# Prompt rows of the experts taken by eight, and the last norm moved into the last expert

## The reference

```
aff  = softmax(h @ router)                       # every token, 16 experts
gate, idx = top_k(aff^T, 2 * t / 16)             # each expert takes 128 of 1024 sample tokens,
                                                 #   16 of 128 prompt tokens
xe   = h[idx]
hid  = silu(xe @ e_gate) * (xe @ e_up)           # 1024 -> 2816
ye   = (hid @ e_down) * gate                     # 2816 -> 1024
x    = x + gt2 * zeros.at[idx].add(ye)
y    = x * rsqrt(mean(x * x) + eps) * final_norm_g
```

## Time and profile before

| | us |
|---|---|
| median of 3 timed runs | 3868.48 (3867.92 to 3871.03) |
| profiled execution | 3860.96 |
| its span, first to last instruction | 3859.2 |

### The profile page before, as it was taken

The page is one execution under the profiler, slowest core; times in us unless marked ns, Lnnn a source line. Parts: engine busy times, 40 slices in busy tenths (PEclk is TensorE's granted clock), DMA queues, the critical chain, the costliest instruction groups (busy, mean ns, idle before and its releaser), DMA issues. The chain is left out here.

```text
span 3859.2 us, 81746 instructions
## 1 busy us (share of the span) xinstructions
PE 3562.1 (92%) x37038; PEld 3101.1 (80%) x37038; DVE 1231.4 (32%) x3103; ACT 671.1 (17%) x1677; POOL 192.0 (5%) x150
## 2 busy tenths in 40 slices
PE   5899899999899979289999999999999999999995
PEld 2387685959555545189999999999999999999995
DVE  3376767777444443701111111111111111111112
ACT  2323324242144532100000000000000000000001
POOL 0010101010000000000000000000000000000000
PEclk7899999999999999589999999999999999999997
DMA  7200000000121022098887878788787878878773
GB/s 323 61 16 10 15 5 20 4 19 4 27 79 31 18 72 94 21 354 292 274 266 263 267 259 273 261 273 268 265 267 258 273 262 269 268 268 269 258 251 110
DMA packets 498393, 664.38 MB, mean 172 GB/s; under 512 B 31183, under 2 KB 437095, under 8 KB 494975
## 3 DMA queue, kind: packets, MB, share of 16 engines
q1 hardware_dynamic: 492238, 640.23, 49.5%
q0 software_dynamic: 5632, 18.88, 1.9%
q10 hardware_dynamic: 176, 0.05, 0.0%
HBM read 630.70 MB, written 28.36 MB: 171 GB/s over the span
## 5 line engine op out<-in xcount | busy, mean ns | idle before, releaser
L2094 PE MATMUL bank<-e_hid,e_wd 128*128 128x144 f32 x5632 | 760.1, 288 | 0.0
L2082 PE MATMUL bank<-e_xT,e_wg 128*128 128x144 f32 x5632 | 749.5, 286 | 1.0 <-ACT e_xT L2136 1.0
L2082 PE MATMUL bank<-e_xT,e_wu 128*128 128x144 f32 x5632 | 748.1, 286 | 0.0
L2082 PEld LDWEIGHTS bank<-e_xT,e_wg 128*128 128x128 f32 x5632 | 715.5, 190 | 1.0 <-issue 1.0
L2094 PEld LDWEIGHTS bank<-e_hid,e_wd 128*128 128x128 f32 x5632 | 710.5, 190 | 5.6
L2082 PEld LDWEIGHTS bank<-e_xT,e_wu 128*128 128x128 f32 x5632 | 714.4, 190 | 0.0
L2179 DVE TENSOR_TENSOR e_tm<-bank,e_sg 128x144 f32<-128x144 f32 x352 | 108.3, 308 | 1853.0 <-ACT e_sg L2143 1853.0
L2143 ACT ACTIVATE e_sg<-bank 128x144 f32<-128x144 f32 x352 | 102.2, 290 | 1998.4 <-PE bank L2082 1998.4
L532 PE MATMUL bank<-hT_x,wblk 128*128 128x512 f32 (+1 forms) x672 | 237.5, 511 | 14.5 <-DMA wblk<-in_w_in 8.5
L532 PEld LDWEIGHTS bank<-hT_x,wblk 128*128 128x128 f32 x672 | 114.1, 197 | 130.4 <-issue 112.4
L727 PE MATMUL bank<-r_TW,r_X 64*64 64x64 f32 x2880 | 167.5, 220 | 4.3 <-DVE r_X L1198 1.3
(11 more groups left out here) (324 smaller groups left out, 3469.9 us busy)
## 6 DMA issues: line engine op xcount, KB each, us to landing
e_wg<-in_e_gate SPq DMA_DIRECT2D x176, 1024.0 KB, 5.5
e_wu<-in_e_up SPq DMA_DIRECT2D x176, 1024.0 KB, 8.1
e_wd<-in_e_down SPq DMA_DIRECT2D x176, 1024.0 KB, 11.0
h_wmod<-in_w_mod SPq DMA_DIRECT2D x24, 1024.0 KB, 17.1
wblk<-in_w_in SPq DMA_DIRECT2D x22, 512.0 KB
h_x<-in_x_sample SPq DMA_DIRECT2D x8, 512.0 KB, 6.6
wo<-in_w_out SPq DMA_DIRECT2D x2, 2048.0 KB, 11.6
o_x<-in_x_sample SPq DMA_DIRECT2D x8, 512.0 KB, 4.2
```

The source lines that it names most:

```text
L2082: last = nc.tensor.matmul(bank[6 + b % 2][:, j * TOK:(j + 1) * TOK], w[s][:, k, f], xT[e % 2][:, k, :], start=(k == 0), stop=(k == KD - 1))
L2094: last = nc.tensor.matmul(bank[k // PER_BANK][:, c:c + TOK], wd[s][:, b % DUO, k * P:(k + 1) * P], hid[:, b % 2, :], start=(b == 0 and k % ...
```

## The change

- `topk` treats the prompt first; SP writes its indices and gates to HBM and loads them back as two columns of 128 (`idxq`, `gateq`): rows of eight experts one below the other.
- The prompt rows are gathered 128 at a time (`gather_prompt`, for experts 0 to 7 and 8 to 15), transposed once into `xpT` (`prompt_token`), and VectorE copies each expert's 16 columns into its `xT` (in `tokens`).
- On the way back `collect` copies an expert's 16 prompt columns into `ypT`; for experts 0 to 7 and 8 to 14 these are turned together (`prompt_output`, in expert 8 and expert 15) and scaled together (`prompt_scaled`). Each expert's 16 rows are still added by a scatter of their own, in a row, each waiting for the one before (`scatter_prompt`).
- Token numbers 0 to 127 compared with the last expert's prompt indices give a 16x128 matrix `pick`; its product with the last expert's 16 prompt rows is added to the prompt tile in place of a scatter.
- The stage `final` is gone. In expert 15, while its products run, SP loads the eight sample tiles (without expert 15's sum) into weight buffers that are free, ScalarE squares them, VectorE norms them in place. POOL gathers the 128 rows that expert 15 chose. When its result is there, these rows are summed and normed, and after the eight tiles are stored they are stored over them by an indirect DMA.

The core of the diff (`topk`'s SP block, buffers, semaphores and the plain halves of changed pairs are left out):

```diff
+        GROUP = ((0, 8), (8, 15))
+        SQUARES = {14: (0, 1), 15: (2, 3), 16: (4, 5), 17: (6, 7)}
+        SCALES = {18: (0, 1), 19: (2, 3), 20: (4, 5), 21: (6, 7)}
...
 SP, behind the last weights:
+                sp.wait_ge(used, FIRST_FREE + 1)
+                sp.wait_ge(sc, 16 * LASTE)
+                for i in range(TILES - 1):
+                    if i == 6:
+                        sp.wait_ge(used, NEXT_FREE + 1)
+                        sp.dma_start(gf, ...).then_inc(gf_in, 16)
+                    sp.dma_start(fx[i], K.dram["ffn"][i * P:(i + 1) * P, :]).then_inc(fx_in[i], 16)
+                sp.wait_ge(scp, 16 * LASTE)
+                sp.dma_start(fx[8], K.dram["ffnp"][:, :]).then_inc(f8_in, 16)
+                for i in range(TILES - 1):
+                    sp.wait_ge(fy_ok, i + 1)
+                    sp.dma_start(A["y_sample"][0, i * P:(i + 1) * P, :], fx[i]).then_inc(fy_st, 16)
+                sp.wait_ge(py_ok, 1)
+                sp.dma_start(A["y_prompt"][0, :, :], fx[8]).then_inc(py_st, 16)
...
 POOL:
+                def scatter_prompt(e):
+                    if e:
+                        K.hold(pool, scp, 16 * e)
+                    pool.indirect_dma_start(out=K.dram["ffnp"][:, :], ..., in_=yp[part(e), :],
+                                            compute_op=ALU.add).then_inc(scp, 16)
...
+                    if e == LASTE:
+                        K.hold(pool, x_ps, NE)
+                        K.hold(pool, sc, 16 * LASTE)
+                        pool.indirect_dma_start(out=xe[:, :], in_=K.dram["ffn"][:, :], ...).then_inc(fr_in, 16)
+                    for g, (first, last) in enumerate(GROUP):
+                        if e == last + 1 or (e == last and last == NE - 1):
+                            K.hold(pool, sp_ok, 2 * g + 2)
+                            for i in range(first, last):
+                                scatter_prompt(i)
...
+                K.hold(pool, scp, 16 * LASTE)
+                K.hold(pool, fy_st, 16 * (TILES - 1))
+                K.hold(pool, zy_ok, 1)
+                pool.indirect_dma_start(out=A["y_sample"]..., in_=xe[:, :], ...).then_inc(patched, 16)
+                K.hold(pool, patched, 16)
...
 TensorE:
-                    nc.tensor.transpose(bank[b][:, c:c + CAP], xe[:, k * P:(k + 1) * P], K.ident[:, :])
-                    last = nc.tensor.transpose(bank[b][:, c + CAP:c + TOK], xp[:, k * P:(k + 1) * P],
-                                               K.ident[0:CAPP, 0:CAPP])
+                    last = nc.tensor.transpose(bank[3 + k // HALF][:, ...], xe[:, k * P:(k + 1) * P], K.ident[:, :])
...
+                        if e == GROUP[0][1] - 1 and b in (2, 3, 4, 5, 9, 10, 11, 12):
+                            prompt_token(1, b - 2 if b < 6 else b - 5, 5)
+                        for g, (first, last) in enumerate(GROUP):
+                            if e == last and b in (4, 5, 6, 7, 10, 11, 12, 13):
+                                prompt_output(g, b - 4 if b < 8 else b - 6)
...
+                for h in range(2):
+                    pe.wait_ge(sp_ok, 2 * len(GROUP) + h + 1)
+                    nc.tensor.matmul(bank[h][:, :], pick[:, :], yp[0:CAPP, h * 512:(h + 1) * 512], ...)
...
 VectorE, in block b of expert e:
+                        if e and b == YT + 2:
+                            collect(e - 1)
+                        for g, (first, last) in enumerate(GROUP):
+                            if e == last and b in (9, 15):
+                                prompt_scaled(g, b // 15)
+                        if e == LASTE:
+                            if b == 17:
+                                mean_square(slice(0, 8), fsq_ok, 8, fms_ok)
+                            if b == 18:
+                                reciprocal(slice(0, 8), frt_ok, frc_ok)
+                            for i in SCALES.get(b, ()):
+                                normed(fx[i], i).then_inc(fy_ok, 1)
...
 VectorE, behind the last expert:
+                V.tensor_tensor(xe[:, :], xe[:, :], ye[:, :], ALU.add).then_inc(z_ok, 1)
+                last_prompt_scaled(0)          # waits for scp at 16 * 15
+                last_prompt_scaled(1)
+                mean_square(slice(9, 10), zsq_ok, 1, zms_ok)
+                reciprocal(slice(9, 10), zrt_ok, zrc_ok)
+                normed(xe[:, :], 9).then_inc(zy_ok, 1)
```

More of the change, by code:

```diff
@@ new lines, in experts, with part @@
+        fx = [cell(n) for n in range(TILES)]
+        gf, fjunk = cell(TILES), [cell(TILES + 1), cell(TILES + 2)]
+        fst = sb("final_stats", [P, 4, TILES + 1])
+        number = sb("token_number", [CAPP, P], I32)
+        numf = sb("token_numberf", [CAPP, P])
+        lastf = sb("last_index", [CAPP, 1])
+        pick = sb("last_pick", [CAPP, P])
+        SQUARES = {14: (0, 1), 15: (2, 3), 16: (4, 5), 17: (6, 7)}
+        SCALES = {18: (0, 1), 19: (2, 3), 20: (4, 5), 21: (6, 7)}
+        def part(e):
+            return slice((e % 8) * CAPP, (e % 8 + 1) * CAPP)
@@ L2104, in output, with output_last_prompt @@
                         pe.wait_ge(yv_ok, e + 1)
[L2105 to L2110, removed]
-                        last.then_inc(y_ps, 1)
+                    last = nc.tensor.transpose(bank[3 + k // HALF][:, (k % HALF) * P:(k % HALF + 1) * P], yT[:, k, 0:CAP],
+                                               K.ident[:, :])
+                    if k % HALF == HALF - 1:
+                        last.then_inc(y_ps, 1)
+                def output_last_prompt(k):
+                    last = nc.tensor.transpose(bank[5 + k // HALF][0:CAPP, (k % HALF) * P:(k % HALF + 1) * P],
+                                               yT[:, k, CAP:TOK], K.ident[:, :])
+                    if k % HALF == HALF - 1:
+                        last.then_inc(yp_ps, 1)
                 for k in range(KD):
                     token(0, k)
+                for k in range(KD):
+                    prompt_token(0, k, 5 - 3 * (k // HALF))
                 gate_up(0, 0)
@@ L2220, in _ @@
                 scaled(NE - 1, 1)
[L2223 to L2277, removed]
-                    V.tensor_scalar(st[:, 1, i:i + 1], st[:, 0, i:i + 1], 1.0 / D, EPS, ALU.mult, ALU.add)\
-                     .then_inc(ms_ok, 1)
-                def out(i):
-                    dve.wait_ge(rt_ok, i + 1)
-                    V.reciprocal(st[:, 3, i:i + 1], st[:, 2, i:i + 1]).then_inc(rc_ok, 1)
-                    dve.wait_ge(rc_ok, i + 1)
-                    if i >= 4:
-                        dve.wait_ge(y_st[i % 4], 16 * (i // 4))
-                    V.scalar_tensor_tensor(y[i % 4][:, :], x[i][:, :], st[:, 3, i:i + 1], gf[:, :], ALU.mult,
-                                           ALU.mult).then_inc(y_ok, 1)
-                mean(0)
-                dve.wait_ge(rows, 16)
-                for i in range(TILES):
-                    if i + 1 < TILES:
-                        mean(i + 1)
-                    out(i)
@@ L2298, in trunk @@
+                for h in range(2):
+                    n = slice(h * 512, (h + 1) * 512)
+                    dve.wait_ge(pick_ps, h + 1)
+                    last = V.tensor_tensor(fx[8][:, n], fx[8][:, n], bank[h][:, :], ALU.add)
+                last.then_inc(p_ok, 1)
+                mean_square(slice(8, 9), psq_ok, 1, pms_ok)
+                reciprocal(slice(8, 9), prt_ok, prc_ok)
+                dve.wait_ge(p_ok, 1)
+                normed(fx[8], 8).then_inc(py_ok, 1)
 def trunk(nc, A):
```

207 lines of the change are left out of this document (177 added, 30 removed).

## The result

The changed kernel takes 3780.55 us (median of 4 runs, 3779.4 to 3781.19), the kernel before 3869.18 beside it (4 runs, 3867.92 to 3871.03): ratio 0.977, interval 0.9753 to 0.9787. That is 88.6 us faster, where 71.4 were forecast.

The account below looks back on a forecast made before the run. TensorE's issue was taken to bound the kernel from first to last product. Experts -55.5 + 2.6, start +1.0 and tail -19.5 sum to -71.4 us, from 3868.48 to 3797; range 3786 to 3828 (own range 3786 to 3806).

Parts of the forecast that it names:

- The bound: From first gate/up product to last down product, time is the sum of what TensorE issues; busy 800 of 800 us.
- E: End of the last down product, 3811.23 us in the profile before; the tail's times count from it.
- 1, TensorE in the experts: Expert loop: transposes removed give -55.5 us, added ones +2.6; an expert takes 131.2 us instead of 134.9.
- 2, the cover: Expert blocks: new VectorE and ScalarE work, squares and norms included, hides under 4.7 us of cover per block, costing nothing.
- 3, the start: Ahead of the first product: the larger prompt gather, transposes and copies cost +1 us (ends -0.5 and +3).
- 4, the tail: Behind the last down product: scatter chain, stores, patch scatter and exit take 28.5 us instead of 48.0, so -19.5.
- the step of the chain: Group 1's seven serial prompt scatters on POOL, each waiting for the one before: 5.5 us a step, low end 3.8.
- C: Scatter chain's end, forecast E + 1.1; also the rival: slow token transpose isn't the 16 rows' doing, 3820 or more, chance 0.07.
- The exit: POOL leaving a block at the end: 0.4 + 5.2 us, the 5.2 paid once in either kernel.
- A: Rival: POOL sees its own DMAs late, 10.8 us a scatter in the tail; 3834 us, chance 0.14.
- B: Rival: the scatter chain runs at the loaded loop's price, 8.5 us a step; 3818 us, chance 0.12.
- D: Rival: slower than before, serial scatters with every store behind them on SP; 3876 us at 16.6 a scatter, chance 0.02.

Follow-up runs that it names:

- experiment 2: Kernel before, each prompt token piece turned from all 128 rows by a product with 16 identity columns instead of a 16-row transpose: 3853.32 us, ratio 0.9962.
- experiment 1: Kernel before, with a small POOL memset behind its last wait in the experts and another as its first instruction of the next stage: 3867.86 us.
- experiment 3: Changed kernel with the old last stage behind the experts, expert 15's prompt rows scattered like the others, no early norms: 3804.64 us, ratio 0.984.
- experiment 6: Changed kernel with fourteen serial scatters, sample stores and chosen rows' norm no longer behind the chain, POOL's wait ahead of the patch dropped: 3796.49 us.
- experiment 4: Changed kernel with the eight sample squares, their statistics and norms put behind the last expert: 3796.81 us, ratio 0.982.
- experiment 7: Changed kernel with six weight duos loaded during top-k, `gt2`/`gt2p` first in the experts, ScalarE's root table loaded early: 3776.16 us, ratio 0.9765.
- experiment 8: As experiment 7, with `gt2` and `gt2p` loaded during top-k too: 3779.6 us, ratio 0.9774.
- experiment 9: The changed kernel again, with no edit: 3781.59 us, ratio 0.9774.
- experiment 5: Changed kernel with a second, zero-adding scatter behind each of group 1's seven prompt scatters, fourteen in a row: 3804.4 us, ratio 0.9838.

## Why the prediction was right or wrong

**The bound: right.** TensorE's issue sets the time from the first product to E. The clock stayed 1.00.

**1, TensorE in the experts: right.** -54.0 against -52.9. The samples' gathers of consecutive experts stand 131.15 us apart (131.2 forecast). The unrounded 0.353 for the 16-row transpose is shown by the changed kernel's blocks (6.35 to 5.99) and loop; experiment 2 shows that 0.09 of it is its neighbour's ahead. That the row count alone makes it dear was argued, not separated.

**2, the cover: right.** TensorE did not idle in expert 15. The last norm ended at E - 0.5 (forecast -0.4), ScalarE's table for the sigmoid was loaded again from 3736.86 on, 0.7 before it was needed. The bare price of squares and norms is 16.3 (20 forecast), since part of it finds other cover behind E.

**3, the start: too dear by 2.9 of -1.9 against +1.** Behind top-k's end the first transpose came at 9.8 (10.9 before), the last one ended at 13.5 (forecast 14.8), and the first product stood 1.6 behind that (forecast 3.1). The forecast added the larger gather to a time at which the old kernel had both kinds of rows; the new one starts on the sample rows as soon as they are there and the prompt's eight transposes follow 1.8 later. And it put all copies in a row behind the last transpose, where VectorE's first (1656.88) and ScalarE's lie beside the transposes; 1.6 are left behind them. The ends given, -0.5 and +3, missed it by 1.4.

**4, the tail: here the prediction failed**, at the step of the chain: "I take 5.5". It measured 3.9 (landing 3.1, wake and issue 0.8). The 4.6 that it was built on is the landing of a scatter issued 1.9 us behind one of 512 KB; "with little beside it" was wrong: behind the 512 KB scatter the small one takes 4.6 to 4.7 in before and experiments 1 to 3, and without one 3.1 in the rows of after. Six steps (25.3 us in all) and a landing put C at E - 8.4 instead of +1.1, and with that what decides changes: no more the stores behind C (E + 6.9) but the chosen rows (E + 8.6, forecast +9.3; issue at 9.4). In numbers, of the 11.3 us from the forecast end at E + 28.5 to 17.2:
- the patch is issued at +9.4 instead of +16.9: 7.5;
- it lands in 3.3 instead of 6.0: 2.7. The 6.0 row is of an accumulating scatter with a second one beside it; the patch is a plain one, alone. In experiment 6 the plain patch landed in 3.5 between a small scatter issued 1.6 us before it and a 512 KB load 1.5 us behind it, which points at the adding and not at the company; no run has the adding scatter alone;
- the exit takes 4.5 behind the landing instead of 5.6: 1.1.

The estimate of 2.2 us a scatter, worked out from the Trainium skill (DMA: Bandwidth & Descriptors, section Anatomy of one DMA), lies 0.9 under the measured 3.1, nearer than the 4.6 that I preferred, and what it made of the tail, that it hangs on the chosen rows, is what the trace shows. The measured row that I set against it was of another situation.

**The exit: right in place.** Experiment 1 shows it for the kernel before. In the changed kernel 4.5 us pass from the patch's landing to the end, in experiments 4, 7, 8 and 9 too (5.1 in 5), and in 6, where POOL is done early, the end follows the last store by 0.5. So it is POOL's, and paid where POOL is last. The prompt's path needs that 0.5 too, and its store lands 1.7 ahead of the changed kernel's end: an estimate from these rows is that a faster patch would give back only 1.2 us before the prompt's path decides.

**The rivals.** A fell by experiment 1 and by the steps of 3.9. B fell by the same rows. Its price was also too high: group 0's prompt scatters, issued in the loaded loop, show it in POOL's timeline of after.

```profile
2959.89 1.35 POOL L2110 DMA_INDIRECT scratch_ffnp<-e_yp,idxp  x1 [0.30 <-issue]
2966.88 1.30 POOL L2110 DMA_INDIRECT scratch_ffnp<-e_yp,idxp  x1 [5.64 <-DMA scratch_ffnp<-e_yp,idxp]
...
3002.08 1.28 POOL L2110 DMA_INDIRECT scratch_ffnp<-e_yp,idxp  x1 [3.63 <-DMA scratch_ffnp<-e_yp,idxp]
```

Seven steps take 42.2 us, 6.0 each (4.0 to 7.9), where 8.5 was said; the 7.6 of the earlier trace rows was of scatters behind 512 KB ones, the same fault as with the 4.6. C fell by the loop's 54.0 and by experiment 2. D was far off: it needed C = +72.5, and fourteen scatters in a row brought C to +19.0.

**The range.** The low bound of the step, 3.8, was written down and was almost the truth, but only 3786 was let in for it. With 3.8 a step, the chosen rows deciding, and a landing of 2.9 for the patch, the tail alone would have been some 10 us lower: 3787, and with the start's -0.5 and the 3 us between runs an end near 3783, still above the 3780.55 measured. The case in which the chosen rows decide was given no chance of its own. Three of the tail's prices (the step, the patch's landing, the exit) were taken from rows of another situation and all lay too high; I treated them as independent. Only for the step is the other situation shown to be the cause.

Still open: what POOL's exit spends 5 us on, and what makes the time ahead of top-k vary by 8 us in equal code (the granted clock over 1000 to 1420 us lies between 0.94 and 0.97 in them).

## What to carry to other kernels

Where TensorE is the bound, a small transpose between full products can cost its neighbours time too: compare the block with and without it, and gather such pieces until they fill the rows. When a step is priced by the nearest row, look first at what ran beside that row, and work out which wait ends last for the low price too: here 1.6 us a step moved the decision to another chain. A serial chain ahead of the last product is free only until its end passes the work that follows; know both times, as experiments 5 and 6 do.

## What the hardware did that I had not expected

- POOL needs 6.4 us from its last instruction in the experts, where it issued DMAs, to the first in the next stage (experiment 1); the change of stage into the experts takes 1.2. At the program's end 4.5 us follow POOL's last landing, and 0.5 SP's where POOL is done early (experiment 6).
- One transpose from 16 rows between products over 128 takes 0.35 us in all, one from 128 rows 0.11, and giving the same 16 columns as a product over 128 rows (mostly zeros) is cheaper: 0.22 to 0.23 (experiment 2).
- Serial scatter-adds of 16 rows mostly run 3.9 us apart when alone (single steps up to 5.0 in experiments 5, 7 and 9), 5.3 and 5.8 beside plain stores (experiment 6) and 6.0 on average beside the weight loads.
- The same 512 KB gather lands in 4.4 us alone (experiment 8) and in 7.3 beside the loads of `gt2` and `gt2p` (experiment 7).
